# Feed-forward up units: the order of the rounded and the remainder product of a bank

## The reference

```
def conv_ffn(x, w_up, conv_w, conv_b, w_down):
    hdn = x @ w_up                       # (256, 1024) @ (1024, 5632)
    hdn = causal depthwise conv of width 3 over the tokens (hdn) + conv_b
    gate, up = jnp.split(hdn, 2, axis=-1)
    return (jax.nn.gelu(gate, approximate=True) * up) @ w_down
```

## Time and profile before

| | |
|---|---|
| median of three runs | 856.09 us (855.87 to 856.25) |
| profiled execution | 856.17 us |
| its span, first to last instruction | 854.4 us |
| granted TensorE clock | 0.998 |
| matmuls in the profile | 5596 |
| of them at lines 2113 and 2116 | 640 and 640 |
| TensorE, VectorE, ScalarE busy | 99%, 80%, 60% of the span |

### The profile page before, as it was taken

The page is one execution under the profiler, slowest core; times in us unless marked ns, Lnnn a source line. Parts: engine busy times, 40 slices in busy tenths (PEclk is TensorE's granted clock), DMA queues, the critical chain, the costliest instruction groups (busy, mean ns, idle before and its releaser), DMA issues.

```text
span 854.4 us, 14686 instructions
## 1 busy us (share of the span) xinstructions
PE 843.5 (99%) x5596; PEld 738.3 (86%) x5596; DVE 679.4 (80%) x1045; ACT 513.6 (60%) x746; POOL 57.8 (7%) x118
## 2 busy tenths in 40 slices
PE   8999999999999999999999999999999999999997
PEld 8999889888888889888898888888889889998885
DVE  6767469898887987566689878888888887699784
ACT  6665656765665684575586655656756867542552
POOL 2233100000000012200010000000000001000000
PEclk9999999999999999999999999999999999999999
DMA  8635326555546447524456465445264154462411
GB/s 336 228 137 186 142 99 216 203 193 204 193 152 229 160 152 251 215 99 148 148 210 247 148 216 201 173 177 216 100 222 148 65 187 148 170 226 82 188 50 50
DMA packets 22521, 147.71 MB, mean 173 GB/s; under 512 B 2864, under 2 KB 3152, under 8 KB 5825
## 3 DMA queue, kind: packets, MB, share of 16 engines
q1 hardware_dynamic: 20448, 140.52, 45.3%
q0 software_dynamic: 1872, 6.37, 2.2%
q10 hardware_dynamic: 144, 0.04, 0.0%
HBM read 145.86 MB, written 1.06 MB: 172 GB/s over the span
## 4 chain that ended last, share of the span: by engine, by line
PE 93%; DVE 2%; ACT 2%; issue 1%; DMA 1%; POOL 0%; POOLq 0%; DVEq 0%; SPq 0%
PE psC L2113 17%; PE psC L2026 11%; PE psC L2028 11%; PE psC L2027 11%; PE psC L2116 9%; PE psD L2026 5%; PE psD L2027 5%; PE psD L2028 5%; PE psC L2143 2%; PE psC L2145 2%; PE psC L2152 2%; PE psD L2440 1%; PE psD L2432 1%; PE psD L2850 1%; PE psD L2472 1%
## 5 line engine op out<-in xcount | busy, mean ns | idle before, releaser
L1164 DVE TENSOR_TENSOR w_lo<-raw,w_hi 128x2048 fp32r<-128x2048 f32 x122 | 278.8, 2288 | 57.1 <-ACT w_hi L583 56.5
L583 ACT ACTIVATE w_hi<-raw 128x2048 fp32r<-128x2048 f32 x125 | 238.4, 1911 | 66.6 <-PE psC L2028 31.0
L2113 PE MATMUL psC<-xT,w_hi 128*128 128x512 f32 x640 | 200.8, 395 | 0.0
L2116 PEld LDWEIGHTS psC<-xT,w_lo 128*128 128x128 f32 x640 | 120.2, 188 | 28.2
L2116 PE MATMUL psC<-xT,w_lo 128*128 128x256 f32 x640 | 125.7, 278 | 0.0
L2113 PEld LDWEIGHTS psC<-xT,w_hi 128*128 128x128 f32 x640 | 98.6, 189 | 1.2
L2026 PE MATMUL psC<-xT,w_hi 128*128 128x256 f32 x304 | 87.1, 287 | 0.1
L2027 PE MATMUL psC<-xT,w_hi 128*128 128x256 f32 x304 | 86.0, 283 | 0.0
L2028 PE MATMUL psC<-xT,w_lo 128*128 128x256 f32 x304 | 86.0, 283 | 0.0
L2026 PE MATMUL psD<-w_hi,oT_hi 128*128 128x512 f32 x208 | 81.1, 390 | 0.0
L2027 PE MATMUL psD<-w_lo,oT_hi 128*128 128x512 f32 x208 | 81.0, 389 | 0.0
(11 more groups left out here) (343 smaller groups left out, 1494.4 us busy)
## 6 DMA issues: line engine op xcount, KB each, us to landing
raw<-stream SPq DMA_DIRECT2D x130, 1024.0 KB, 4.8
gbc<-post_g POOLq DMA_DIRECT2D x6, 512.0 KB, 4.4
arena<-first SPq DMA_DIRECT2D x4, 512.0 KB, 5.4
arena<-f_rows POOLq DMA_DIRECT2D x4, 512.0 KB, 8.5
h<-x_in SPq DMA_DIRECT2D x2, 512.0 KB, 9.4
out<-h SPq DMA_DIRECT2D x3, 256.0 KB, 2.1
arena<-b_in POOLq DMA_DIRECT2D x1, 640.0 KB, 6.0
out<-h SPq DMA_DIRECT2D x2, 128.0 KB, 2.0
```

The source lines that it names most:

```text
L583: nc.scalar.activation(w_hi[:, slot, :], raw[:, raw_slot, :], ACT.Copy).then_inc(hi_done, 1)
L1164: V.tensor_tensor(w_lo[:, slot, :], raw[:, raw_slot, :], w_hi[:, slot, :].bitcast(F32), ALU.subtract).then_inc(lo_done, 1)
L2113: MM(psC[:, up_bank(e, a), :], hi[:, k, a * P:a * P + P], xT[:, kk_, :, :].rearrange("p i t -> p (i t)"), start=(kk_ == 0), stop=False, sk ...
L2116: ins = MM(psC[:, up_bank(e, a), 0:T], lo[:, k, a * P:a * P + P], xT[:, kk_, 0, :], start=False, stop=(kk_ == KT - 1), skip_group_check=True)
```

## The change

In each tile k of x, up_wide issued the two rounded products of a pair of banks and then the two remainder products. Now it issues, for one bank, the rounded and the remainder product, and then the same for the other bank. The second loop header goes; the instructions themselves, their operands and the semaphores stay.

```diff
                     for k in range(4):
                         kk_ = 4 * half + k
                         for a in pair:
                             MM(psC[:, up_bank(e, a), :], hi[:, k, a * P:a * P + P], xT[:, kk_, :, :].rearrange("p i t -> p (i t)"),
                                start=(kk_ == 0), stop=False, skip_group_check=True)
-                        for a in pair:
                             ins = MM(psC[:, up_bank(e, a), 0:T], lo[:, k, a * P:a * P + P], xT[:, kk_, 0, :], start=False,
                                      stop=(kk_ == KT - 1), skip_group_check=True)
                     if half and pair[0] == 0:
                         ins.then_inc(half_done, 1)
```

## The result

The changed kernel takes 859.96 us (median of five runs) against 856.09 us. One of the five took 1507.04 us at a mean granted clock of 0.753 and is left out of the comparison; the other four, 859.74 to 860.05 us, give a ratio of 1.0044, 95% interval 1.0032 to 1.0057. Its profiled execution took 859.96 us too, with a span of 858.2 us, 3.8 more than the 854.4 of the earlier trace rows. It is slower by more than the 0.2% that a measurement can tell, and outside the forecast range of 855.0 to 858.3 us.

What follows compares the result with a forecast made beforehand. TensorE, never idle in the feed-forward stretches, was taken as the bound. Four terms of 0 and +0.9 us for width changes gave 857.1 us on the profiled execution's 856.17, forecast as 857.0, range 855.0 to 858.3.

Steps and rivals of the forecast that it cites:

- work: Up_wide's products: the same columns and the same weight loads in both orders, 0.
- hand-overs: Semaphore counts on a bank pair's last product: ScalarE, VectorE and the next weight split released after the same products, 0.
- same bank: In up_wide, a narrow product adding to columns its wide one has just written: no charge beyond its width, 0.
- weight loads: In up_wide, a load of 114 ns fits behind a narrow product's 120 ns slot, in either order: 0.
- changes of width: In up_wide, four changes per four products instead of two: 2.9 ns more for each of 320 fours, 0.93 us.
- The alternating stream of 384 and 128 columns: Lines 2472 and 2473: 286.7 ns a pair, read as alternation costing nothing beyond the streams alone; change would return 0.93 us.
- rival A: Up_wide's excess over single-width streams goes or does not move: 855.2 to 856.1 us; chance 0.37.
- lower bound: Up_wide's width-change term at its lowest: alternation costs nothing and the 2.9 ns per four returns, -0.9 us.
- The upper bound of the term: Up_wide's width-change term at its highest: the existing 2.9 ns per four added once more, +0.9 us.
- Rival B: In up_wide, a weight load behind a lone narrow product comes late: 353 ns a pair, up to 859.2 us; chance 0.15.
- C: In up_wide, a narrow product directly behind a wide one is cheap, 113 ns: 5.2 us less, 850.9 us; chance 0.06.
- The sign of being wrong: Up_wide's wide and narrow product in one bank spaced more than 3 ns off the sum of the two alone.

Runs made afterwards that it cites:

- experiment 1: Kernel before the change, with the two narrow (256-column) products of each four swapped, so one follows its own bank's wide product: span 854.5 us, ratio to before 0.9999.
- experiment 2: Against the kernel before: widths in turn for six of eight pairs, narrow product one tile late and in the other bank: span 856.1 us, ratio 1.0021.
- experiment 7: Changed kernel with the narrow product added to its bank's second half, span 858.4 us; or the wide product cut into two of 256 columns, 862.2 us.
- experiment 4: Changed kernel with the remainder product at 384 columns instead of 256: span 892.2 us, 406.6 ns a pair.
- experiment 5: Changed kernel with all up-unit products 512 columns wide, span 921.5 us; or with widths kept and all weights from w_hi, 858.2 us.
- Experiment 3: Against the kernel before (runs of two, span 854.4 us): runs of one width of three, four or eight products: spans 855.0, 856.5 and 854.7 us.
- Experiment 6: Changed kernel with 384, 448, 480 or 496 columns beside 256: spans 829.7, 842.2, 846.9, 850.5 us; 512 beside 448: 911.9 us.

## Why the prediction was wrong

**Right:** the points "work", "hand-overs", "same bank" and "weight loads". TensorE has no idle time in either stretch, nothing else moved, and experiments 1, 2 and 7 show that the bank is not what costs, experiment 4 that a late load is not.

**Wrong: the term "changes of width", point 5 of the sum.** It says that changes of width are what costs, and this much the runs show (experiments 1, 2 and 5). Its price failed. I took 2.9 ns for the two changes of W W N N and added as much again for two more, so that a four would have 5.8 ns of excess; measured is 12.8 (two pairs at 6.4). The term was to be 0.93 us and came to 3.8: 3.1 in the up units, and 0.75 in the down units right behind them, which the sum did not have at all. Three assumptions failed.

- The price is not fixed per change. Experiment 3 has 3 to 16 ns for a change and its return, without a simple rule in the length of the run. The trace before could have warned: there the single entry into 512 columns at 758.83 us costs some 20 to 30 ns, not 1.4.
- The alternating stream of 384 and 128 columns, from which I read that alternation may cost nothing, could not speak for 512 columns. Experiment 6 shows that alternation with up to 496 columns has indeed no price in itself. I took this stream for the lower bound, and much of the nearly four tenths of the chance for rival A rested on it.
- A cost need not fall inside the products that cause it. A fifth of this one falls on the down products.

The upper bound of the term, +0.9, was the doubled value of a pattern with runs of two, and no row supported it as a bound.

**Rival B** gave 353 ns a pair and 859.2 us, close to the 353.1 and 860.0, and the chunk of 22.6 us that I had named as its mark is what the changed kernel shows (22.60). So this check pointed to B, whose cause was not the right one: the load has room, and a narrow product of 384 columns with ample room pays the same. B's price rested on the starts 235 ns behind a wide product inside the mix. In the changed kernel starts behind a wide product do lie 0.23 to 0.24 us apart, but that the price came out right with a wrong cause is luck as far as the runs show.

**Rivals A and C** fell. The early starts of narrow products (C) are paid back, as argued.

**The sign of being wrong** that I had given, a pair more than 3 ns over the sum of the two alone, came (6.4). The only cause that I allowed for it, full-width results added to at once over half of their columns, did not: the excess is there when N goes to another bank (experiment 2) or to the half that was written last (7), and putting N behind the W of its own bank in runs of two adds nothing (1).

**Open:** what in TensorE or its way to PSUM makes 512-column products beside shorter ones slow. It is neither the bank, nor the half of it, the weight tile, the tile of x, or room for the load. Whether the full bank as target or the 512 columns as stream is what counts could not be separated here, since both came together in every run. Why runs of two are cheaper than runs of three and four is open too, and why 22 of 80 alternating sequences in experiment 2 are nearly free of the excess. No order tried beat the kernel before; the kernels with 384 to 496 columns are shorter because they compute less.

## What to carry to other kernels

Where TensorE never waits, the order of products with different widths is itself a cost: 512-column products beside 256-column ones lost 1.5 to 6.4 ns a pair by order alone. Equal widths lost none, and widths of up to 496 lost none among themselves. Price a new order from a stream with the same widths and the same run length; a stream of other widths, or a price per change scaled up, can miss it, here by a factor of four. Measure such spacings from start to start over tens of products, and look also at what follows the stretch, where a fifth of the loss appeared.

## What the runs showed of the hardware that I had not expected

- A step between 496 and 512 columns: in alternation with 256-column products, 340.0 ns a pair at 496, 353.1 at 512.
- An excess beside 512 columns that does not shrink as the widths draw near: 6.4 and 6.6 ns with 256 and 384 columns, 11.0 with 448, and none at 512.
- A transient behind a change to 512 columns: eight take 1.84 us instead of 1.81 after a run of eight of 256, and a down projection of 24 takes 5.47 us instead of 5.44 after 496 and 256 in turn.
- The same alternation in two rhythms within one kernel (experiment 2): about 347 ns a pair in 22 sequences, 351 to 352 in 58.
